# Split operands for the mixer's recurrence projection, and the forget product ahead of it

## What is computed

```python
h = rmsnorm(x, mix_norm[l])                      # x: 256 tokens x 1024
z = h @ w_in[l]
q, k, v, f_logit, gate_in, rec_in = jnp.split(z, split_points, axis=-1)   # 512, 512, 512, 8, 512, 512 columns
log_f = jax.nn.log_sigmoid(f_logit + b_forget[l])
att = forgetting_attention(q, k, v, log_f)       # adds differences of cumsum(log_f) to the logits
rec = causal_depthwise_conv(rec_in, conv_w[l], conv_b[l])
rec = rg_lru(rec, w_a[l], b_a[l], w_x[l], b_x[l], lru_lambda[l])
lru_out = rec * jax.nn.gelu(gate_in, approximate=True)
x = x + jnp.concatenate([att, lru_out], axis=-1) @ w_out[l]
```

## Time and profile before

| | us |
|---|---|
| median of 3 runs | 1332.69 |
| lowest and highest | 1331.86, 1337.57 |
| the profiled execution | 1334.59 |
| its span | 1332.0 |

### The profile page before, as it was taken

One profiled execution on the slowest core, in us unless ns is written; L12 is line 12 of the kernel. 1 busy time (PEld: TensorE's weight loads), 2 busy tenths in 40 slices (PEclk: granted clock), 3 DMA queues, 4 the chain that ended last, 5 costly groups with the idle time before them and its releaser, 6 DMA issues. The chain is left out here.

```text
span 1332.0 us, 19658 instructions
## 1 busy us (share of the span) xinstructions
PE 1289.1 (97%) x8066; PEld 1001.5 (75%) x8066; DVE 656.7 (49%) x1128; ACT 577.2 (43%) x938; POOL 66.4 (5%) x88
## 2 busy tenths in 40 slices
PE   6999999999999999999999999999999999999996
PEld 2767777776778888879877889997877666666663
DVE  2313765486443443467576776667545542222212
ACT  2447444554662232347655567443475411111112
POOL 0000010242000000000001330000000000000000
PEclk9999999999999999999999999999899899999998
DMA  9523022234432242315423213553371489999990
GB/s 384 224 103 151 32 95 96 95 127 180 169 113 86 93 156 91 127 65 200 158 95 127 96 65 127 199 213 114 126 284 64 166 313 411 397 421 396 418 367 34
DMA packets 34655, 239.07 MB, mean 179 GB/s; under 512 B 4480, under 2 KB 4736, under 8 KB 6656
## 3 DMA queue, kind: packets, MB, share of 16 engines
q1 hardware_dynamic: 34560, 237.74, 46.2%
HBM read 236.68 MB, written 1.05 MB: 178 GB/s over the span
## 5 line engine op out<-in xcount | busy, mean ns | idle before, releaser
L238 DVE TENSOR_TENSOR pieces_lo<-weight_ring,pieces_hi 128x1024 fp32r<-128x1024 f32 x156 | 192.3, 1237 | 239.2 <-ACT pieces_hi L230 238.7
L256 PE MATMUL proj<-h_hi,pieces_hi 128*128 128x512 f32 (+1 forms) x800 | 283.6, 355 | 2.8 <-PEq L551 1.7
L258 PE MATMUL proj<-h_hi,pieces_lo 128*128 128x512 f32 (+1 forms) x800 | 276.0, 345 | 0.0
L257 PE MATMUL proj<-h_lo,pieces_hi 128*128 128x512 f32 (+1 forms) x800 | 274.7, 343 | 0.0
L230 ACT ACTIVATE pieces_hi<-weight_ring 128x1024 fp32r<-128x1024 f32 x156 | 163.4, 1053 | 140.3 <-PE score L258 96.6
L256 PEld LDWEIGHTS proj<-h_hi,pieces_hi 128*128 128x128 f32 x800 | 151.0, 189 | 30.0 <-issue 10.7
L257 PEld LDWEIGHTS proj<-h_lo,pieces_hi 128*128 128x128 f32 x800 | 151.4, 189 | 21.3 <-issue 2.2
L258 PEld LDWEIGHTS proj<-h_hi,pieces_lo 128*128 128x128 f32 x800 | 150.8, 189 | 19.7
L256 PE MATMUL score<-l_y_hi,pieces_hi 128*128 128x512 f32 (+1 forms) x192 | 65.2, 340 | 0.9 <-DVE l_merged L1430 0.7
L256 PE MATMUL proj<-pieces_hi,h_hi 128*128 128x512 f32 x160 | 65.1, 407 | 0.0
L258 PE MATMUL score<-l_y_hi,pieces_lo 128*128 128x512 f32 (+1 forms) x192 | 64.9, 338 | 0.0
(11 more groups left out here) (482 smaller groups left out, 2353.2 us busy)
## 6 DMA issues: line engine op xcount, KB each, us to landing
weight_ring<-in_stream SPq DMA_DIRECT2D x110, 1024.0 KB, 4.9
expert_parts<-in_experts SPq DMA_DIRECT2D x35, 1024.0 KB, 10.3
expert_parts_behind<-in_experts SPq DMA_DIRECT2D x35, 1024.0 KB, 10.7
weight_ring<-in_experts SPq DMA_DIRECT2D x26, 1024.0 KB, 11.7
l_rows<-in_rows SPq DMA_DIRECT2D x2, 768.0 KB, 16.4
l_y_attn<-in_ada_first SPq DMA_DIRECT2D x1, 1024.0 KB, 5.4
l_y_gla<-in_ada_first SPq DMA_DIRECT2D x1, 1024.0 KB, 7.5
l_y_sgu<-in_ada_first SPq DMA_DIRECT2D x1, 1024.0 KB, 8.4
```

What stands on the lines that cost most here:

```text
L238: eng.tensor_tensor(self.part(self.lo_ring[:, n % NPIECE, :], kind), self.raw(slot, c, kind), self.part(self.hi_ring[:, n % NPIECE, :], ki ...
L256: pe.matmul(out, sh, mh, start=start, stop=False)
L257: pe.matmul(out, sh, ml, start=False, stop=False)
L258: return pe.matmul(out, sl, mh, start=False, stop=stop)
```

## The change

`rec` becomes a split projection like the others: its four pieces of weights come first in `MIXER_PIECES`, and PE does 96 fp32r matmuls in the place of 32 float32 ones. `f` stands ahead of `rec` on PE. Its follow-up work on ACT and DVE becomes a step of its own, `fs`, behind `rec`'s last piece. SP's code is the same; what it waits for before it loads `k` is now DVE's split of `rec`'s last piece.

```diff
-MIXER_PIECES = [(n, j) for n in ("q", "k", "v", "gat") for j in range(4)]
+MIXER_PIECES = [(n, j) for n in ("rec", "q", "k", "v", "gat") for j in range(4)]
...
-    steps = [("norm", t) for t in range(2)] + [("turnx", i) for i in range(4)] + [("hsplit", i) for i in range(4)]
-    steps += w("q", 0) + [("rec", 0)] + w("q", 1) + [("rec", 1)] + w("q", 2) + [("rec", 2), ("rec", 3)]
-    steps += [("f", 0), ("q", 0)] + w("q", 3) + [("q", 1)] + w("k", 0) + [("q", 2)] + w("k", 1) + [("q", 3)]
+    steps = [("norm", t) for t in range(2)] + [("turnx", i) for i in range(4)] + w("rec", 0) + [("hsplit", 0), ("hsplit", 1)]
+    steps += [("hsplit", 2), ("hsplit", 3)] + w("rec", 1, 2) + [("f", 0), ("rec", 0)] + w("rec", 3) + [("rec", 1)] + w("q", 0)
+    steps += [("rec", 2)] + w("q", 1) + [("rec", 3)] + w("q", 2) + [("fs", 0)]
+    steps += [("q", 0)] + w("q", 3) + [("q", 1)] + w("k", 0) + [("q", 2)] + w("k", 1) + [("q", 3)]
...
                     acc = PT.open(pe, J("f"))
                     for k in range(KT):
+                        if k % 2 == 0:
+                            pe.wait_ge(*PJ.evacuated(J("turnx", k // 2)))
                         last = pe.matmul(acc[0:8, 0:T], par[:, M_WF + 8 * k:M_WF + 8 * k + 8], hT[:, k, :],
                                          start=(k == 0), stop=(k == KT - 1))
...
-                elif kind in ("q", "k", "gat"):
+                elif kind in ("rec", "q", "k", "gat"):
...
-                        if (kind, i) == ("q", 0) and k % 2 == 0:
+                        if (kind, i) == ("rec", 0) and k % 2 == 0:
                             pe.wait_ge(*sig.x_h_lo.at(k // 2 + 1))
...
-                elif kind == "rec":
-                    w = slot(kind)
-                    acc = PJ.open(pe, J(kind, i))
-                    for k in range(KT):
-                        if (kind, i) == ("rec", 0) and k % 2 == 0:
-                            pe.wait_ge(*PJ.evacuated(J("turnx", k // 2)))
-                        last = pe.matmul(acc[:, 0:T], w[:, k, i * P:(i + 1) * P], hT[:, k, :],
-                                         start=(k == 0), stop=(k == KT - 1))
-                    last.then_inc(*PJ.done())
-                    used(kind, PJ.ready(J(kind, i)))
...
-                elif kind == "f":
+                elif kind == "fs":
                     act.wait_ge(*PT.ready(J("f")))
...
-                elif kind == "f":
+                elif kind == "fs":
                     dve.wait_ge(*sig.fsoft.at(1))
```

More of the change, by code:

```diff
@@ L1594, in raw_piece @@
             w = W.both(f"x.{name}").rearrange("p (k c) -> p k c", c=512)
-            return w[:, :, j * P:(j + 1) * P] if name in ("q", "k", "gat") else w[:, 2 * j:2 * j + 2, :]
+            return w[:, :, j * P:(j + 1) * P] if name in ("rec", "q", "k", "gat") else w[:, 2 * j:2 * j + 2, :]
         def split_piece(ring, name, j):
             x = ring[:, MIXER_PIECES.index((name, j)) % NPIECE, :]
-            return x.rearrange("p (k c) -> p k c", c=P if name in ("q", "k", "gat") else 512)
+            return x.rearrange("p (k c) -> p k c", c=P if name in ("rec", "q", "k", "gat") else 512)
         def piece_split(name, j):
```

## The result

| | us |
|---|---|
| before, median of 19 executions (lowest, highest) | 1334.45 (1330.57, 1338.89) |
| after, median of 19 executions (lowest, highest) | 1338.86 (1333.21, 1344.16) |
| after over before, with 95% interval | 1.0029 [1.0018, 1.0040] |
| the profiled execution after, and its span | 1335.57, 1333.8 |

The change makes the kernel 0.29% slower, 3.9 us (4.0 between the means of the executions, 4.4 between the medians). The whole interval lies within 0.5%, so by the bound of the prediction it counts as the same. The table of before further up has the median of three executions, 1332.69; over 19 it is 1334.45. The profiled execution after is the second fastest of its 19, and only 1.0 us slower than the profiled one of before (1334.59). So the traces show the steps of the change; the size of the loss at the end comes from the many executions.

What follows compares the result with a forecast made beforehand. TensorE, busy 97% of the span, was taken as the bound: 930.6 + 3.55 + 8 x 2.93 put `cum` 1.7 us later, the clock added 1.65, so 1332.7 + 3.3 = 1336.0 us, range 1331.5 to 1340.

Steps and rivals of the forecast that it cites:

- the bound of the prediction: Whole kernel: a measurement can tell about 0.5% (6.7 us) from no change; less counts as the same.
- The wait: Ahead of `f`: TensorE waits for `par_in` until 930.6, idle 4.3 us where it stood 0.33 before.
- rival 4: Ahead of `f`: no wait, `f` starts at 926.64, `cum` at 953.6, the 2.3 us trade kept, 1330.4; chance 0.07.
- The clock: Behind the idle ahead of `f`: the clock falls to half for 3.3 us, costing 1.65 us.
- Rival 1: Around `f`: the clock doesn't fall, only the 1.7 us remain, 1334.4; chance 0.14.
- rival 2: Around `f`: the clock stays low for 6.5 us, costing 3.25 us, 1337.6; chance 0.14.
- rival 3: At `f` and `rec`: `f` doesn't bring the clock back, 10.4 us low, 5.2 lost, 1339.6; chance 0.06.
- The trade of `rec`: `rec`'s product on TensorE: split form takes 11.71 us in place of 13.98, giving back 2.27 us.
- VectorE and `fs`: Around `fs`: the piece for `q`'s last quarter takes 8.2 us, needed after 8.8; 0.6 to spare, cost 0.
- rival 5: At `fs`: its wait is late and `q`'s last quarter stands, 1 to 2 us on top, 1337 to 1338; chance 0.09.
- The step from `cum` to the end: Behind `cum`: a microsecond of TensorE in the mixer is one at the end, so 3.3 us later at both.
- Time outside the span: Profiled execution: span from 1332.0 to 1335.3, and from 1334.6 to 1337.9 in all.

Runs made afterwards that it cites:

- e1: The changed kernel measured again with no edit; 1.0021 of before, 2.6 us slower.
- e2: The changed kernel with the 64 columns of `f`'s weights moved into the second DMA of `small_in`, only `cum` waiting for `par_in`; 0.9969 of before, 3.9 us faster.
- e3: The changed kernel with nine unused float32 products on TensorE filling the wait ahead of `f`, the wait left; 1.0002 of before, 0.0 us.
- e5: The kernel before with `f` first, `rec` plain, and `f`'s weights early as in e2; 1.0012 of before, 2.1 us slower.
- e4: The kernel before with only the order changed, `f` first and its follow-up behind a plain `rec`; 1.0039 of before, 5.1 us slower.
- e12: The kernel before with `cum` in two halves, the second behind `k`'s first piece; 0.9996 of before, 0.9 us faster.
- e8: e2 with three unused float32 products on TensorE ahead of `f`; 0.9971 of before, 3.9 us faster.
- e7: e2 measured again; 0.9976 of before, 3.6 us faster.

## Why the prediction was right

It forecast 3.3 us more (1336.0) and called it the same; measured were 4.0 and 2.6 us more. The absolute 1338.86 lies 2.9 us above the forecast, because the three executions that it started from had a median 1.8 us below that of 19, and the rest, 1.1 us, is the size of the change (4.4 between the medians). By its own steps:

| step | predicted | after | e1 |
|---|---|---|---|
| first DMA to start of `f` | 930.6 - 923.19 = 7.41 | 7.19 | 7.27 |
| TensorE idle ahead of it | 4.3 | 4.06 | 4.15 |
| `f`, with the clock's part | 3.55 + 1.65 | 4.84 | 5.23 |
| `rec` and `q`, eight pieces | 8 x 2.93 = 23.44 | 23.22 | 23.23 |
| first DMA to `cum` | 36.05 | 35.25 | 35.73 |
| `cum` later than before | 3.3 | 2.6 | 3.0 |

- **The wait**, the term that decided the sign, was right to 0.25 us, and so was the rule it rests on, that a landing counts from the start of the issue. In after the later DMA is issued at 923.26 + 0.45 and lands 5.8 us on, 929.5; `f` starts at 929.59 (5.8 is the longest landing of L1950 in that trace). e2 shows that nothing else would have held `f` up for more than 0.22 us. It is also the case that rival 4 describes: the prediction put its `cum` at 953.6, 30.4 us behind the first DMA, and the trace has 30.12.
- **The clock** fell, as it had behind the idle time ahead of 1053.72. The low stretch is 3.4 us long (928.8 to 932.2; predicted 3.3), 0.75 of it idle time that costs nothing, so it costs 1.3 us in after, and 1.7 in e1, where it began when `f` was running. Rival 1 (no fall), rival 2 (6.5 us long) and rival 3 (the clock isn't back within `f`) are out: the clock was back before `f` ended, in both traces. e3 prices the whole term at 1.3 to 1.8 us at `cum`.
- **The trade of `rec`**: 2.27 us predicted, 2.29 between e5 and e2. The pieces run at 2.90 us each; weight loads fill the queue in split form. The Trainium skill (FP8 and Floating Point Precision, "TensorE Precision Notes") counts four passes for a true float32 product; three products in their place would have saved 3.5 us by that count, and neither pair of traces shows that.
- **VectorE and `fs`**: the margin was 0.6 us by the sum. In the trace the piece for `q`'s last quarter is done at 953.07 + 1.2 = 954.3, and TensorE comes to it at about 934.43 + 7 x 2.90 = 954.7: 0.4 us. Nothing stands; rival 5 is out. It is thin cover: VectorE waits 1.24 us for ScalarE's chain just ahead of it.
- **The step from `cum` to the end** is the weak one. The prediction held that a microsecond in the mixer is one at the end. No run bears that out to the microsecond: from `cum` on the mixer took 94.95 us before, 93.03 after and 94.67 in e1, and the experts 281.2 against 283.1 twice. In the trace of after the two differences, -1.9 and +1.9, cancel, and in e1 only the +1.9 stays. e5 is the plain counterexample, sooner at `cum` and slower at the end. That two measurements of the changed kernel, 4.0 and 2.6 us, lie on both sides of 3.3 is therefore in part luck. The prediction named such low stretches "behind `cum`" and put 1.65 us on each; it did not look at the router, where one costs 1.9 and where the trace of before had the better of the two cases.
- **Time outside the span**: I took the 2.6 us of before over; after, it is 1.7 to 1.9 us in all 19 executions. Over all executions its mean is 2.5 in before, e4 and e5, 1.5 in e12 and 1.8 to 1.9 in all others. So 0.7 us in the comparison of before with a split kernel is no work of the mixer or the experts, and within the span, where the 3.3 were worked out, the changed kernel loses more than the totals say: 3.4 us in e1, and 4.7 in the first measurement by the same 0.7 (an estimate from these means). What sets it is open.

The forecast said that it fails if the stretch behind `cum` or the experts change by more than 2 us. In the trace of after both changed by 1.9, so it holds by a hair.

## What to carry to other kernels

When a step is moved to the front of a block, look first at when its operands land, not at how long it runs: here 32 KB in the wrong one of four DMAs cost 4 us of waiting and 1.3 to 1.7 of clock, more than the arithmetic saved by the rest of the change, and moving those 64 columns turned a loss of 0.2 to 0.3% into a gain of 0.3%. Here 4 us of idle TensorE cost their own length and then 1.3 to 1.7 us more by the clock, and idle products bought the second part back (e3). And where two versions differ by less than the low stretches of the clock can move (some 2 us here, each), read the term from a trace and the verdict from many executions, and don't expect the two to agree by the microsecond.

## What the runs showed of the hardware

- The same 32 router records take 4.3 to 4.7 us or 7.0, by where the low clock stands. A little work put in 130 us earlier went with it: e8 and e2 differ by 1.3 us of idle products ahead of `f`, and their experts by 2.9 us, in one trace of each.
- The idle time ahead of the experts is nearly the same in both cases, 2.93 us before and 3.0 after, and TensorE works without a longer gap behind it; yet the low clock lasted 3.4 us in one before it came back, and 13.7 in the other. So idle time ahead is not all that decides, and no experiment here separated what does.
- A kernel made a microsecond longer (e8 against e2) had the same mean, within 0.8 us of standard error, and its executions scattered three times as wide. The narrow width of e2, 2.6 us, came back in e7 with 2.9, on another chip, where the others with twelve executions have 3.7 to 8.3.
